# Attention units and q/k/v projections of one transformer mixer run in turn, in a two-block kernel on one core

## The reference, cut to what matters

```
def odd_mixer(x, w_in, w_out, cos, sin):
    q, k, v = jnp.split(x @ w_in, 3, axis=-1)          # 1024 -> 3 x 1024, 16 heads of 64
    q = partial_rope(heads(q), cos, sin) * (DL_HEAD_DIM ** -0.5)
    k = partial_rope(heads(k), cos, sin)
    v = heads(v)
    for (w, d) in DL_PAIRS:                            # three dilated causal windows
        o, lse = dilated_branch(q, k, v, d, w // d)
        ...
    wts = jax.nn.softmax(jnp.stack(lses, axis=0), axis=0)
    o = jnp.einsum('gbhs,gbhsd->bhsd', wts.astype(v.dtype), jnp.stack(outs, axis=0))
    return o.transpose(0, 2, 1, 3).reshape(B, S, D) @ w_out
```

## Time and profile before

| | |
|---|---|
| median of 3 runs | 4297.63 us |
| profiled execution | 4307.66 us |
| its span in the trace | 4305.9 us |
| TensorE matmul busy | 3780.9 us, 88% |
| VectorE busy | 2115.9 us, 49% |
| ScalarE busy | 1501.9 us, 35% |
| granted TensorE clock, mean | 0.924 |
| projections of the odd mixer | 3501.8 to 3651.3 us from the span's start |
| attention of the odd mixer | 3651.3 to 3811.0 us |

### The profile page before, as it was taken

How to read it: one execution, slowest core, us unless ns; L and a number is a source line. 1 busy time by engine, 2 the same in 40 slices (tenths; PEclk the granted TensorE clock), 3 DMA queues, 4 the chain that set the end, 5 groups by cost and what they waited for, 6 DMA issues and landing times.

```text
span 4305.9 us, 59574 instructions
## 1 busy us (share of the span) xinstructions
PE 3780.9 (88%) x24624; PEld 2900.2 (67%) x24624; DVE 2115.9 (49%) x3456; ACT 1501.9 (35%) x2684; POOL 161.4 (4%) x408
## 2 busy tenths in 40 slices
PE   7888889999995877788768999896999999679999
PEld 4644466777883556778627888575788777457886
DVE  3355544333447573566354445635444554535445
ACT  4333434122224472233243333333333342434333
POOL 0000000000000010333110000000000000000000
PEclk9989999999996998899879999795999999789999
DMA  4011112232111554566412222110123222012221
GB/s 178 31 64 53 40 39 88 108 127 108 59 59 51 153 150 153 143 158 162 117 70 77 99 97 107 40 71 25 69 88 107 90 76 88 1 44 88 99 97 59
DMA packets 295293, 380.57 MB, mean 88 GB/s; under 512 B 240496, under 2 KB 243440, under 8 KB 260336
## 3 DMA queue, kind: packets, MB, share of 16 engines
q1 hardware_dynamic: 281648, 330.88, 23.9%
q10 hardware_dynamic: 13376, 45.87, 2.9%
HBM read 331.61 MB, written 45.11 MB: 87 GB/s over the span
## 4 chain that ended last, share of the span: by engine, by line
PE 73%; DVE 11%; ACT 7%; DMA 3%; issue 2%; POOL 2%; SPq 1%; ACTq 0%; DVEq 0%; POOLq 0%
PE ps L253 17%; PE ps L254 17%; PE ps L255 17%; PE ps L327 4%; PE ps L720 2%; PE ps L701 2%; PE ps L1188 1%; PE ps L1190 1%; PE ps L1189 1%; DMA s_it<-rt 1%; DVE mx L1441 1%; DVE nsm L793 1%; ACT s L3192 1%; DVE xml L1446 1%; PE ps L3156 1%
## 5 line engine op out<-in xcount | busy, mean ns | idle before, releaser
L238 ACT ACTIVATE whi<-panel 128x1024 fp32r<-128x1024 f32 (+1 forms) x524 | 442.2, 844 | 667.0 <-PE ps L255 631.3
L245 DVE TENSOR_TENSOR wlo<-panel,whi 128x1024 fp32r<-128x1024 f32 (+1 forms) x524 | 503.8, 963 | 331.5 <-ACT whi L238 322.2
L253 PE MATMUL ps<-xh,whi 128*128 128x512 f32 x1184 | 481.2, 406 | 43.4 <-DVE xl L2359 23.0
L253 PE MATMUL ps<-dh,whi 128*128 128x512 f32 (+1 forms) x1280 | 474.9, 371 | 0.0
L254 PE MATMUL ps<-dh,wlo 128*128 128x512 f32 (+1 forms) x1280 | 472.7, 369 | 0.0
L255 PE MATMUL ps<-dl,whi 128*128 128x512 f32 (+1 forms) x1280 | 470.9, 368 | 0.0
L254 PE MATMUL ps<-xh,wlo 128*128 128x512 f32 x1184 | 466.4, 394 | 0.0
L255 PE MATMUL ps<-xl,whi 128*128 128x512 f32 x1184 | 465.3, 393 | 0.0
L253 PE MATMUL ps<-hh,whi 128*128 128x512 f32 (+1 forms) x960 | 351.6, 366 | 26.7 <-DVE hl L447 26.7
L254 PE MATMUL ps<-hh,wlo 128*128 128x512 f32 (+1 forms) x960 | 339.3, 353 | 0.0
L255 PE MATMUL ps<-hl,whi 128*128 128x512 f32 (+1 forms) x960 | 338.8, 353 | 0.0
(11 more groups left out here) (448 smaller groups left out, 5964.5 us busy)
## 6 DMA issues: line engine op xcount, KB each, us to landing
panel<-in_w SPq DMA_DIRECT2D x248, 1024.0 KB, 4.8
ld<-s_fe ACTq DMA_DIRECT2D x16, 1024.0 KB, 6.9
s_fe<-x SPq DMA_DIRECT2D x37, 256.0 KB, 2.8
ld<-s_fe ACTq DMA_DIRECT2D x24, 256.0 KB, 4.6
ld<-s_fe ACTq DMA_DIRECT2D x8, 768.0 KB, 6.9
vv<-s_fe ACTq DMA_DIRECT2D x24, 256.0 KB, 7.0
s_fe<-x SPq DMA_DIRECT2D x40, 128.0 KB, 2.3
s_ys<-yy SPq DMA_DIRECT2D x16, 256.0 KB, 3.2
```

Of the source, the lines that this page charges most:

```text
L238: e.activation(unit(u)[0][:, 0:kc, :], w, ACT.Copy).then_inc(*w_hi.up(u))
L245: e.tensor_tensor(lo[:, 0:kc, :], w, hi[:, 0:kc, :].bitcast(F32), SUB).then_inc(*w_lo.up(u))
L253: e.matmul(out, hi[:, k, :], xh, start=k == 0, stop=False)
```

## The change

The two parts are merged into one list of steps, `OSTEPS`, which all three engines walk through, each doing its share of a step. A step is one of three kinds: ("p", t) a projection tile, ("r", t) its turn, ("a", n) an attention step. The attention step n means the scores of unit n and the transposes and v product of unit n-2 on TensorE, soft(n-1) and the copies of n-2 on ScalarE, the masking of n and soft(n-1) on VectorE.

Panels and tiles now come by group: tile t belongs to group t // 6 and is q, q, k, k, v, v of it. Attention units run over g outside and qb inside. The attention of group g takes turns with the projection tiles of group g+1; the last group's attention has tiles only up to its beginning. `Q8`, `K8` and `V8` hold two groups, and group g writes where g-2 was, after waits for g-2's last readers.

PSUM is divided anew: scores use banks 0 and 1 (before 0 to 3), transposes 2 and 3, the v product bank 4 alone, projection tiles banks 5 and 6, turns bank 7 alone. The third and fourth score of a unit wait for VectorE to have masked the first and second.

The split of the output into high and low parts is spread over the last attention steps, and `odo`'s first tile waits for its parts one by one.

```diff
-    LUNITS = [(g, qb) for qb in range(4) for g in range(4)]
+    LUNITS = [(g, qb) for g in range(4) for qb in range(4)]
...
+    OSTEPS = [("p", 0), ("p", 1), ("r", 0), ("p", 2), ("r", 1), ("p", 3), ("r", 2), ("p", 4), ("r", 3), ("p", 5), ("r", 4)]
+    for _g in range(2):
+        _n, _t = 4 * _g, 6 * _g + 6
+        OSTEPS += [("a", _n), ("r", _t - 1), ("p", _t), ("p", _t + 1), ("r", _t), ("a", _n + 1), ("r", _t + 1), ("p", _t + 2),
...
     def odd_pe(e):
...
+        def tile(t):
+            if t > 1:
+                e.wait_ge(*od_ac.at("tile", t - 2))
+            x = hsrc(OXH, OXL, MAIN)
+            pe_tile(e, OU + t, B[5 + t % 2][:, :], x if t else ffn0.tail.parts(e, 0, x)).then_inc(*od_mm.up("unit", OU + t))
...
         def scores(n):
             g, qb = LUNITS[n]
             nk = qb * P + P
+            if qb == 0:
+                for i in range(4):
+                    e.wait_ge(*od_dv.at("rope", 6 * g + i))
             for i in range(4):
...
-                if n:
-                    e.wait_ge(*dl_dv.at("score", n - 1, i))
...
+                if 4 * n + i > 1:
+                    e.wait_ge(*dl_dv.at("score", (4 * n + i - 2) // 4, (i - 2) % 4))
...
-        for n in range(18):
-            if n < 16:
-                scores(n)
-            if n > 1:
-                out(n - 2)
-        e.wait_ge(*od_dv.at("lo", 7))
+        for kind, i in OSTEPS:
+            if kind == "p":
+                tile(i)
+            elif kind == "r":
+                turn(i)
+            else:
+                if i < 16:
+                    scores(i)
+                if i > 1:
+                    out(i - 2)
         pj_odo.pe(e)
...
     def odd_dve(e):
...
+        for kind, i in OSTEPS:
+            if kind == "p":
+                dve_lo(e, OU + i + 2)
+            elif kind == "r":
+                turn(i)
+            else:
+                if i < 16:
+                    scores(i)
+                if 0 < i <= 16:
+                    soft(i - 1)
```

More of the change, by code:

```diff
@@ L123, in _panels @@
         if l == 1:
-            out += [((a, j), "odd", 8) for a in ("oq", "ok", "ov", "odo") for j in range(4)]
+            out += [((a, j), "odd", 8) for j in range(4) for a in ("oq", "ok", "ov")]
+            out += [(("odo", j), "odd", 8) for j in range(4)]
         out += mlp("f1", "f2", l, f"ffn{l}")
@@ L3094, in program @@
     ffn1 = Ffn(1, od_dv)
-    pj_odo = Proj(OU + 24, od_mm, od_ac, od_dv, lambda sg: hsrc(OXH, OXL, sg), [MAIN], alpha_add, ffn1.n1, (ffn1.f0,))
-    LUNITS = [(g, qb) for qb in range(4) for g in range(4)]
+    pj_odo = Proj(OU + 24, od_mm, od_ac, od_dv, lambda sg: hsrc(OXH, OXL, sg), [MAIN], alpha_add, ffn1.n1, (ffn1.f0,),
+                  lambda k: od_dv.at("lo", k))
+    LUNITS = [(g, qb) for g in range(4) for qb in range(4)]
     LBASE = [sum(LUNITS[x][1] + 1 for x in range(n)) for n in range(16)]
-    def odd_pe(e):
-        def rope(t):
-            e.wait_ge(*od_ac.at("tile", t))
[L3102 to L3124, removed]
@@ new lines, in program, with is_v, od_before, od_q @@
+    ROTS = [t for kind, t in OSTEPS if kind == "r"]
+    def is_v(t):
+        return t % 6 > 3
+    def od_before(t):
+        if is_v(t):
+            return t - 6
+        return t - 2 if t % 6 > 1 else t - 4
+    def od_q(t):
+        g, i = t // 6, t % 6
+        return (Q8 if i < 2 else K8)[g % 2][:, i % 2, :]
+    def odd_pe(e):
+        def tile(t):
[3 more added lines that the diff above has]
+            pe_tile(e, OU + t, B[5 + t % 2][:, :], x if t else ffn0.tail.parts(e, 0, x)).then_inc(*od_mm.up("unit", OU + t))
+        def turn(t):
+            i = ROTS.index(t)
+            if i > 0:
+                e.wait_ge(*od_dv.at("v" if is_v(ROTS[i - 1]) else "sin", ROTS[i - 1]))
+            e.wait_ge(*od_ac.at("tile", t))
+            if is_v(t):
+                for b in range(4):
+                    x = e.transpose(B[7][:, b * P:b * P + P], OVT[t % 2][:, b * P:b * P + P], ID)
+            else:
+                x = e.matmul(B[7][:, :], PERM[1], OTQ[2 * (t % 2)][:, :], start=True, stop=True)
+            x.then_inc(*od_mm.up("turn", t))
@@ L3173, in odd_act, with tile @@
         act_hi(e, OU + 1)
-        for t in range(24):
+        def tile(t):
             e.wait_ge(*od_mm.at("unit", OU + t))
[L3176 to L3185, removed]
+            if od_before(t) >= 0:
+                e.wait_ge(*od_mm.at("turn", od_before(t)))
+                if not is_v(t):
+                    e.wait_ge(*od_dv.at("rope", od_before(t)))
+            dst = OVT[t % 2] if is_v(t) else OTQ[2 * (t % 2)]
+            e.activation(dst[:, :], B[5 + t % 2][:, :], ACT.Copy).then_inc(*od_ac.up("tile", t))
             act_hi(e, OU + t + 2)
@@ L3230, in rope @@
             e.tensor_tensor(d, d, b, ADD).then_inc(*od_dv.up("rope", t))
[L3232 to L3243, removed]
         def scores(n):
@@ L3268, in soft, with low @@
                     *dl_dv.up("prob", n, i))
[L3270 to L3277, removed]
+        def low(k):
             e.wait_ge(*od_ac.at("hi", k))
             e.tensor_tensor(OXL[:, k, :], OOM[:, k, :], OXH[:, k, :].bitcast(F32), SUB).then_inc(*od_dv.up("lo", k))
+        for kind, i in OSTEPS:
+            if kind == "p":
+                dve_lo(e, OU + i + 2)
+            elif kind == "r":
+                turn(i)
+            else:
+                if i < 16:
+                    scores(i)
+                if 0 < i <= 16:
+                    soft(i - 1)
+                if i > 14:
+                    for k in ((0, 1), (2, 3), (4, 5))[i - 15]:
+                        low(k)
+        low(6)
+        low(7)
         pj_odo.dve(e)
```

96 lines of the change are left out of this document (62 added, 34 removed).

## The result

The changed kernel takes 4313.1 us (median of 6 runs, 4309.05 to 4321.85), the kernel before 4294.47 us on the same chip (6 runs): ratio 1.0044, 95% interval 1.0031 to 1.0058. It is 18.6 us slower; 14.7 were forecast, 4312 us against a first median of 4297.63.

A forecast was written before the change was run, and what follows sets the result against it. TensorE, busy 88% of the span, was taken as the bound. Attention at full clock, added wait included, -24.7 us and the clock +39.4 gave +14.7: 4312 us against 4297.63, forecast 4303 to 4325, wider range 4281 to 4336.

The forecast's parts named there:

- part 2: Attention steps: third score waits for VectorE's mask, behind a tile's low part; TensorE idles 47 us (25 to 60).
- part 3: Attention waits that go or stay: with the added wait, 135 us at full clock against 159.7, so -24.7 us.
- the division's wait: TensorE's wait for VectorE's divided probabilities: over before TensorE arrives in interleaved steps; 6 us left in the last four.
- The v product's wait: In attention, each v product waits for ScalarE's last copy: 16 x 0.85 = 14 us, staying.
- part 4: TensorE's clock falls behind thirteen idle stretches, 2.8 us each, plus 3 in the last steps: +39 us (9 to 62).
- The sum: Whole kernel: -24.7 + 39.4 = +14.7 us, giving 4312 us against the median of 4297.63.
- the clock that holds: Rival, chance 0.17: TensorE's clock does not fall behind the stretches, or only briefly, 0.7 us each; -14, 4284 us.
- only long stretches counting: Rival, chance 0.20: only TensorE's six idle stretches of 3.3 us and more cost clock, 2.8 each; -5, 4293 us.
- the one that was slower still: Rival, chance 0.15: low clock takes most of the next projection tile, 4.5 us a stretch; +37, 4334 us.

The follow-up runs named there:

- e1: Changed kernel with VectorE's mask ahead of the waiting turn and the low part of tile t+2: 4272.65 us, ratio 0.9935 to the kernel before.
- e6: Changed kernel with only the low part of tile t+2 moved behind the masks, the turn keeping its place: 4274.15 us, ratio 0.9946 to the kernel before.
- e2: Changed kernel with scores of units of one or two key blocks packed two to a bank: 4297.28 us, ratio 0.9992 to the kernel before.
- b1: Kernel before with only its scores put in two banks instead of four: stage 349.4 us against 309.2, ratio 1.0093.
- e3: Changed kernel with unread fp32 matmuls ahead of the third score's wait, units 0 to 11 and 13: 4286.7 us, ratio 0.9973 to the kernel before.
- b2: Kernel before with unread fp32 matmuls ahead of the wait for the divided probabilities: stage 292.1 us against 309.2, ratio 0.9960.

## Why the prediction was right

**The bound and the new wait** (part 2): 47 us in thirteen stretches were forecast, 2.9 behind a tile and 4.1 behind a turn. Measured 41.4 + 2.3 us, 2.4 to 2.8 and 3.5 to 3.7 a stretch. Some 0.3 us of the difference is the start of the mask, which I set behind the end of the low part where VectorE's instructions overlap. I counted unit 0 among those directly behind a tile, though the turn of a v tile stands between, as for unit 13; the two measured 2.8 and 2.75, so little hung on it. That the cause is the low part's place was forecast and is shown by e1 and e6. That the two banks are needed for it too is shown by e2, where 22.9 us of these waits went with the low part where it was. The Trainium skill ("Trainium Kernel Development and Optimization", section "Best Practices") names PSUM that ran out as a possible reason for consistent bubbles, and here giving up two of four score banks alone cost 40 us (b1). That was the larger surprise: the prediction treated the banks only as the reason for a wait between the tiles.

**Waits that go and stay** (part 3): the division's wait went as forecast, 39.8 to 0.2. The v product's wait was put at 14, the profile has 12.4 of idle time. The output projection starts without a gap, as forecast.

**The clock** (part 4): 39 us were forecast. e3 measured 28.7 and left a clock of 0.98, which over 297.7 us is some 12 us at half clock, worth 6 at most: 29 to 35, so the term was too large by 4 to 10. The single stretch was read rightly, the tile's head at 0.43 us a matmul, and so was that one stretch passes without a fall (unit 4). But thirteen stretches do not cost thirteen times a fixed price: in e2 four of fifteen went, with 9.2 us of waits, and the clock stayed. The rule of the Trainium skill ("TensorE: Matmul & The Clock Gate", section "Why this matters for your kernels"), to leave no idle gaps between bursts of matmuls, speaks of longer gaps than most of these; with the gaps filled, both orders agree with it: the clock rose from 0.86 to 0.98 (e3) and from 0.85 to 0.97 (b2).

**The sum** came out at +14.7 and the stage at +17.2, because a clock term that was too large stands against a schedule that was too short. Without the clock I had 309.2 - 24.7 = 284.5 us; e3 shows 297.7, or 292 at least if its last half-clock time is taken off. One part of the 7 to 13 us that were missing shows in the rows by line: TensorE is busy with scores for 31.9 us in e3 and for 24.0 in b2, both at nearly full clock, 7.9 more for the same scores now that each unit's four scores run as two bursts; I had put 5 for that. How much of it lies on the path was not tested, and the rest is open. The right total rests in part on two errors of opposite sign, and to that extent on luck; that the change would lose, and by which wait, does not.

**The rivals**: the clock that holds (4284) and only long stretches counting (4293) fall by the total, and by the half clock behind the 2.83 us of unit 0; the one that was slower still (4334) falls by the total.

## What to carry to other kernels

When work of two kinds is made to take turns, write down for each in-order engine what stands ahead of the one instruction that the busiest engine waits for: here a weight's low part, which hangs on the tile just finished, stood ahead of a mask whose input was ready, and moving it alone was worth 38 us of the stage and 39 to 44 of the total (e6). Buffers given up to make room (two PSUM banks) are a change of their own, to be timed alone before the interleaving is judged. Ask of an interleaving what it does at equal clock, too: filling the idle time of both orders showed here that the changed one was no shorter even then. Compare the changed stage, not two single spans, when the effect is of the size of the scatter elsewhere.

## What was not expected of the hardware

Filling TensorE's idle time with matmuls that nobody reads made both orders faster, by 28.7 and 17.1 us of stage, at clocks of 0.98 and 0.97 instead of 0.86 and 0.85. Taking away 9.2 us of all waits (60.2 to 51.0) in e2 left the clock at 0.85, and taking away 8.6 more (42.4) in e1 brought it to 0.94. The mean clock of the stage does not follow the sum of the idle time.
